# Residual x copied into the PSUM accumulators of the experts by ScalarE, in place of TensorE's products with the identity

## The reference: a two-layer trunk with mixture-of-experts mixers

```python
def hierarchical_moe(x, w_router_group, w_router_expert, w_gate, w_up, w_down):
    # top-1 of 4 groups, then top-2 of the 8 experts in it -> combine (tokens x 32)
    for e in range(N_EXPERTS):                                   # 32
        h = jax.nn.silu(t @ w_gate[e]) * (t @ w_up[e])           # 1024 -> 512
        out = out + combine[:, e:e + 1] * (h @ w_down[e])        # 512 -> 1024
    return out

for l in range(DEPTH):                                           # 2
    x = x + mixer(rms_norm(x, norm_mix[l]))
    x = x + hierarchical_moe(rms_norm(x, norm_ffn[l]), ...)      # the residual x
return rms_norm(x, norm_final)
```

## Time and profile before

| | |
|---|---|
| time, median of 3 runs | 1127.88 us (1126.49 to 1129.06) |
| the profiled execution's own time | 1127.11 us |
| its span, first to last instruction | 1125.4 us |
| PE busy / weight load busy | 842.9 us (75%) / 692.4 us (62%) |
| DVE busy / ACT busy | 281.5 us (25%) / 199.0 us (18%) |
| DMA | 438.56 MB, mean 390 GB/s; about 429 GB/s in most slices |
| mean granted TensorE clock | 0.902 of full speed |

### The profile page before, as it was taken

One profiled execution on the slowest core, in us unless ns is written; L12 is line 12 of the kernel. 1 busy time (PEld: TensorE's weight loads), 2 busy tenths in 40 slices (PEclk: granted clock), 3 DMA queues, 4 the chain that ended last, 5 costly groups with the idle time before them and its releaser, 6 DMA issues.

```text
span 1125.4 us, 29787 instructions
## 1 busy us (share of the span) xinstructions
PE 842.9 (75%) x13613; PEld 692.4 (62%) x13614; DVE 281.5 (25%) x692; ACT 199.0 (18%) x372; POOL 5.2 (0%) x31
## 2 busy tenths in 40 slices
PE   5999798576576776687479998886676676675884
PEld 5888776455455554566379987775555555554762
DVE  5666521011010110121157644120110110110111
ACT  5574311000000000000163331110000000000001
POOL 1000000000000000000000000000000000000000
PEclk9999899989988888899979997898888898989897
DMA  9963999999999999999997469999999999999995
GB/s 337 415 229 143 381 421 429 429 429 429 429 429 428 429 428 429 428 428 425 407 390 299 165 235 391 428 429 429 429 429 429 429 429 428 429 428 429 427 426 214
DMA packets 46075, 438.56 MB, mean 390 GB/s; under 512 B 5424, under 2 KB 6988, under 8 KB 20940
## 3 DMA queue, kind: packets, MB, share of 16 engines
q1 hardware_dynamic: 44444, 437.07, 93.2%
q10 hardware_dynamic: 1584, 0.79, 0.3%
HBM read 436.80 MB, written 1.05 MB: 389 GB/s over the span
## 4 chain that ended last, share of the span: by engine, by line
DMA 62%; PE 31%; DVE 3%; ACT 2%; issue 1%; ACTq 0%; SPq 0%; DVEq 0%
DMA ring<-in_w_up 54%; PE psum L1142 9%; PE psum L1281 8%; PE psum L1174 4%; DMA ring<-in_odd_w_in 4%; DMA ring<-in_w_down 3%; PE psum L1288 3%; PE psum L1313 2%; PE psum L1157 2%; PE psum L1296 1%; ACT ring_halves L479 1%; PE psum L1357 1%; DMA ring<-in_even_w_in 1%; PE psum L1108 1%; PE psum L1302 0%
## 5 line engine op out<-in xcount | busy, mean ns | idle before, releaser
L1281 PE MATMUL psum<-ring,m 128*32 128x128 f32 x7936 | 300.2, 316 | 198.4 <-DMA ring<-in_w_up 102.3
L1281 PEld LDWEIGHTS psum<-ring,m 128*32 128x32 f32 x7936 | 261.9, 128 | 242.7 <-DMA ring<-in_w_up 118.2
L1019 DVE TENSOR_TENSOR m<-psum,m 128x128 f32<-128x128 f32 x64 | 18.7, 292 | 591.8 <-ACT m L627 591.8
L1288 PE MATMUL psum<-ring,m 128*32 128x256 f32 x1984 | 121.6, 386 | 27.4 <-DMA ring<-in_w_down 27.2
L1142 PE MATMUL psum<-scr_halves,ring_halves 128*128 128x256 f32 x768 | 108.2, 289 | 4.4 <-DVE hn_halves L731 3.7
L1142 PEld LDWEIGHTS psum<-scr_halves,ring_halves 128*128 128x128 f32 x768 | 102.7, 198 | 5.2 <-DVE ring_halves L702 4.0
L627 ACT ACTIVATE m<-psum 128x128 f32<-128x128 f32 x64 | 17.8, 278 | 496.2 <-PE psum L1281 496.2
L1288 PEld LDWEIGHTS psum<-ring,m 128*32 128x32 f32 x1984 | 64.1, 110 | 66.0 <-issue 32.8
L1313 PE MATMUL psum<-m,hn 128*128 128x96 f32 x704 | 92.5, 295 | 12.6 <-ACT m L629 9.5
L1313 PEld LDWEIGHTS psum<-m,hn 128*128 128x128 f32 x704 | 88.8, 208 | 17.6 <-ACT m L629 14.2
L1296 PE MATMUL psum<-m 32*128 32x256 f32 x1056 | 83.3, 427 | 4.5 <-issue 3.5
(11 more groups left out here) (174 smaller groups left out, 484.4 us busy)
## 6 DMA issues: line engine op xcount, KB each, us to landing
ring<-in_w_gate SPq DMA_DIRECT2D x62, 2048.0 KB, 40.6
ring<-in_w_up SPq DMA_DIRECT2D x62, 2048.0 KB, 40.7
ring<-in_w_down SPq DMA_DIRECT2D x62, 2048.0 KB, 39.3
ring<-in_odd_w_in SPq DMA_DIRECT2D x6, 2048.0 KB, 20.7
ring<-in_even_w_in SPq DMA_DIRECT2D x4, 2048.0 KB, 16.7
ring<-in_even_w_out SPq DMA_DIRECT2D x2, 2048.0 KB, 20.0
spare<-in_w_down SPq DMA_DIRECT2D x2, 2048.0 KB, 16.9
ring<-in_odd_w_out SPq DMA_DIRECT2D x2, 2048.0 KB, 16.2
```

The source lines that it names most:

```text
L1281: last = pe.matmul(GU[CAP * part:CAP * (part + 1), lo:lo + FP], block_of(k), w_of(k)[:, FP * part:FP * (part + 1)], start=k == 0, stop=k = ...
L1288: last = pe.matmul(YB[CAP * part:CAP * (part + 1), 0:DP], hhT[:, CAP * f:CAP * (f + 1)], w[:, f, DP * part:DP * (part + 1)], start=f == 0, ...
```

## The change

ScalarE writes x into banks 0 to 3 with two activations (Copy) per layer, one for each token tile, behind its copies of line 522 and ahead of the Exp table's load. TensorE's eight identity products per layer are gone. A new semaphore `seeded` counts the copies: TensorE waits for it ahead of the loop over the experts, and SyncE ahead of the load that overwrites x.

```diff
@@ SyncE, experts(l)
                 sp.wait_ge(logits_ready, l + 1)
+                sp.wait_ge(seeded, TT * (l + 1))
                 load_early(l, 1)
@@ ScalarE, norm(n), n odd
                         last = act.activation(hT[:, k, :], bank[4 + j][:, kk * S:(kk + 1) * S], ACT.Copy,
                                               scale=gains[:, n, k:k + 1])
                     last.then_inc(hT_act, 1)
+                for t in range(TT):
+                    act.activation(psum[:, 0:NP, DP * t:DP * (t + 1)], x[:, t, :].rearrange("p (c d) -> p c d", c=NP),
+                                   ACT.Copy).then_inc(seeded, 1)
                 preload(ACT.Exp)
@@ TensorE, norm(n)
                 pe.wait_ge(hn_dve, TT * n + 1)
                 turn(0)
-                if n % 2:
-
-                    pe.wait_ge(x_ready, TT * n)
-                    for t in range(TT):
-                        for part in range(NP):
-                            pe.matmul(bank[part][:, DP * t:DP * (t + 1)], ident[:, :], x[:, t, DP * part:DP * (part + 1)],
-                                      start=t == 0, stop=False, skip_group_check=True)
                 pe.wait_ge(hn_dve, TT * n + 2)
                 pe.wait_ge(hn_act, n + 1)
                 turn(1)
@@ TensorE, moe(l)
                 gather(l, 0)
                 pe.wait_ge(xg_ready, after_chunk(l, 0, CHUNKS - 1))
+                pe.wait_ge(seeded, TT * (l + 1))
                 with pe.Fori(0, TURNS) as T:
```

More of the change, by code:

```diff
@@ L199, in trunk @@
         gate_ready = sem("gate_ready")
-        o_ready = sem("o_ready")
+        o_ready, seeded = sem("o_ready"), sem("seeded")
         pc_ready, pc_taken = sem("pc_ready"), sem("pc_taken")
```

## The result

The changed kernel takes 1133.8 us (median of 7 runs, 1131.83 to 1134.42), the kernel before 1127.88 us (7 runs beside them, 1124.75 to 1129.06). The ratio is 1.0052, with a 95% interval of 1.0039 to 1.0065: 5.9 us slower. The forecast was 1132.3 us. The profiled execution took 1133.92 us, its span is 1132.2 us (1125.4 before).

A forecast was written before the change was run, and what follows sets the result against it. DMA was taken as the bound, dry before each layer's first expert. Earlier transposes, slower router and transposes gave +2.6 us per layer: 1127.11 + 5.2 = 1132.3 us, range over the cases 1126.5 to 1134.5.

The forecast's parts named there:

- The bound: Mixer through router and gather to first expert: DMA runs dry there, so each us more counts once per layer.
- What goes: Second transposes on TensorE: without the identity products they start 0.56 us earlier in layer 0, 0.50 in layer 1.
- ScalarE's copies at no cost: Ahead of the Exp table: two copies per layer, 1.05 us each, hidden in 2.4 us of waiting, cost 0.
- The clock: TensorE idle before the second transposes: clock falls 2.7 to 5.1 us after dense work, nearly all the router at 0.50.
- The price of it: Router at half clock takes 6.9 us, 3.2 more, transposes up to 0.2 more; net +2.6 us per layer (+2.3 to +2.8).
- The gather: Gather before the first expert: no change taken, 1.3 us each way per layer kept for the range.
- That the clock would hold: Idle time before the router: clock stays up, the saving stands alone, 1126.05 us; chance 0.15.
- that it would fall in one layer alone: Router: clock falls early in one layer only, +2.6 - 0.5 = +2.1, 1129.2 us; chance 0.11.
- The dearer rival: Slower router pushes gather or first expert further into half clock, 3.2 us more per layer, 1138.7 us; chance 0.04.
- That ScalarE becomes the bound: ScalarE's copies would take over 4.5 us; at 6 us 3 us are lost, 1129.1 us without the clock's fall; chance 0.02.

The follow-up runs named there:

- the kernel with neither: The changed kernel without ScalarE's copies and the waits for them, the identity products still gone: 1134.88 us, ratio 1.0056 to the kernel before.
- products and copies together: The changed kernel with the eight identity products put back, ScalarE's copies and both new waits kept: 1127.0 us, ratio 0.9996 to the kernel before.
- a pause of 1.5 us: The changed kernel with three useless filling products per layer ahead of the second transposes: 1128.72 us, ratio 1.0004 to the kernel before.
- With the pause filled: The changed kernel with six useless products in TensorE's idle time in both layers: 1127.6 us, ratio 0.9992 to the kernel before.
- all waits filled: The changed kernel with six useless products in the idle time, six behind the router and three behind the ranks: 1124.08 us, ratio 0.9964 to the kernel before.
- in layer 0 alone: The changed kernel with six useless products in the idle time of layer 0 only: 1128.69 us, ratio 1.0015 to the kernel before.

## Why the prediction was right, step by step

**The bound** (each us on the path from mixer to first expert counts once): right as far as DMA is dry. The rows, first the kernel before, then the changed one (the earlier trace rows has the load at 138.89, the result above the one at 143.49):

```profile
113.17 1.23 DVE L694 TENSOR_TENSOR x<-psum,x 128x1024 f32<-128x1024 f32 x1 [1.05 <-PE psum L1174]
666.88 1.23 DVE L694 TENSOR_TENSOR x<-psum,x 128x1024 f32<-128x1024 f32 x1 [1.25 <-PE psum L1174]
693.88 0.35 SPq L298 DMA_DIRECT2D ring<-in_w_gate  x1
...
113.98 1.23 DVE L698 TENSOR_TENSOR x<-psum,x 128x1024 f32<-128x1024 f32 x1 [1.04 <-PE psum L1171]
672.34 1.22 DVE L698 TENSOR_TENSOR x<-psum,x 128x1024 f32<-128x1024 f32 x1 [1.21 <-PE psum L1171]
701.10 0.34 SPq L298 DMA_DIRECT2D ring<-in_w_gate  x1
```

From the start of DVE's second addition to the first ring load the path grew from 138.89 - 113.17 = 25.72 to 143.49 - 113.98 = 29.51 us in layer 0, by 3.8; in layer 1 by 1.8 (from 693.88 - 666.88 = 27.00 to 701.10 - 672.34 = 28.76). That makes 5.6; lost DMA time makes 5.4, the medians 5.9. The other 1.2 us of the spans' difference of 6.8 lie outside these two paths; 0.8 of it is there at 113.17 already, ahead of anything that was changed. By layer the forecast was off in DMA's loss: 3.4 and 4.6 us forecast, 4.6 and 4.1 measured, since the gather was longer in layer 0 and shorter in layer 1.

**What goes**: 0.56 and 0.50 us forecast. From DVE's second addition to the second transposes it is 118.31 - 113.98 = 4.33 us, where it was 4.84: 0.51. ScalarE's half of hn was ready at 116.95 + 1.22 = 118.17, and the transposes started 0.14 us later, where the forecast had put 0.06.

**ScalarE's copies at no cost**: right. 1.04 us each, over at 122.4, and shown by putting the products back and by leaving both out.

**The clock** (it falls before the router): right in both layers, at 119.65 and 676.0. My bounds of 2.7 to 5.1 us after the last dense work held: 4.8 and 2.8. The rule of the Trainium skill (TensorE: Matmul & The Clock Gate, HAM oscillation), that work behind a pause of TensorE starts cold, held from the first transpose on in three of the five traced cases with a pause of 3.5 us, all in layer 1. In layer 0 the transposes behind the pause ran at full clock in the changed kernel (1.07 us) and partly so in the kernel with neither (1.77 us); the router behind them was at half clock in all five. Without a pause over 0.5 us ahead of them 8 of 13 traced routers took 3.73 us and 5 took 3.88 to 4.76: the work that keeps the clock up through the transposes doesn't always keep it up through the router.

**The price of it**: the router at 6.9 us as forecast. In layer 0 the transposes were at full clock, in layer 1 at half. The first rank product came 129.68 - 113.98 = 15.70 us behind DVE's addition and 688.40 - 672.34 = 16.06 in layer 1, against 12.96: +2.7 and +3.1, where I had +2.6, with +2.3 and +2.8 as ends. Layer 1 lies 0.3 us past my end: its transposes ran wholly at half clock, and the router started 678.40 - 672.34 = 6.06 us behind DVE's addition and not 4.33 + 1.25 = 5.58, 0.5 us later, where I had put 0.2.

**The gather** at no change: true of the sum alone. It took 6.92 for 5.88 in layer 0 and 5.80 for 7.16 in layer 1: +1.0 and -1.4, within the 1.3 us each way that I had kept for it, but for 0.1. This spread need not be the change's: with products and copies together, where the router is as before, it took 6.30 and 5.68 us. And the prediction misread one row: 7.16 us is not between 3.81 and 7.07, the gather of layer 1 ran at half clock nearly to its end.

So the mechanism was right and the size too: 4.4 us above the median forecast, 5.9 measured. Of the difference 0.8 us is that the sum began at the profiled run's time and not at the median.

**The rivals.** That the clock would hold (0.15) and that it would fall in one layer alone (0.11) are refuted for this pause by five of five routers. With a pause of 1.5 us, though, the second came true in one trace. The dearer rival, the first expert at half clock, did not come: its products took 3.70 us as before. That ScalarE becomes the bound is refuted by the run with both.

What stays open: whether the 0.5 us per layer that the copies free can be had at all. With the pause filled, the kernel is at 0.9992 with an interval that holds both no gain and the 1.1 us; with all waits filled the DMA bound hides them.

## What to carry to other kernels

Work that TensorE does while it would only wait can be worth more than it costs: before it is moved to an idle engine, read the granted clock of the products behind it, and take those at half clock into the sum. What stands behind the pause decides the price, here 16 small products on the one path that DMA waits for. And a shorter path buys only what the bound behind it had lost: count the time for which the loads were dry, 3.3 us here (4.1 to 4.7 were won, each give or take 1.4), before hoping for more.

## What the runs showed that I had not expected

The clock is not a fixed function of the instructions: up to the router of layer 0 the kernels with six products in both layers and in layer 0 alone are the same, with 0.25 and 0.22 us of idle time ahead of the second transposes, and the router took 4.76 us in one and 3.73 in the other. Six dense products right behind the router still ran partly at half clock (4.16 us for six that take 2.86 at full clock elsewhere). Products of no use, placed in two waits of each layer, made the kernel before some 4 us faster (1124.04 us), and one copy of 128x1024 from SBUF into four banks of PSUM cost ScalarE 1036 ns, against 1010 ns for one that reads them.
